# Four banks for the first expert product, the second kind's h2 rows from SBUF, expert numbers a block sooner, and one V row per 1.42 blocks

## The reference, cut to what matters

```python
q = (hc @ wq).reshape(T, PEER_HEADS, 2, PEER_KEY_DIM)
...
v1, i1 = lax.top_k(s1, PEER_TOPK)
v2, i2 = lax.top_k(s2, PEER_TOPK)
...
u_g = exp_u[e]
act = jax.nn.gelu(jnp.einsum('td,thkd->thk', hc, u_g).astype(jnp.float32), approximate=False)
w = (g * act).astype(hc.dtype)
return jnp.einsum('thk,thkd->td', w, exp_v[e])
```

## Time and profile before

| | us |
|---|---|
| median of 3 runs (819.38 to 820.77) | 820.61 |
| the profiled execution's own time | 820.81 |
| its span | 819.0 |
| PE matmul busy | 787.0 (96%) |
| DVE busy | 544.3 (66%) |
| GpSimd busy | 246.6 (30%) |
| ACT busy | 213.8 (26%) |
| chain that ended last: PE | 71% |
| chain that ended last: DMA | 21% |
| moved by DMA: 294.31 MB, mean rate | 359 GB/s |

### The profile page before, as it was taken

The page is one execution under the profiler, slowest core; times in us unless marked ns, Lnnn a source line. Parts: engine busy times, 40 slices in busy tenths (PEclk is TensorE's granted clock), DMA queues, the critical chain, the costliest instruction groups (busy, mean ns, idle before and its releaser), DMA issues.

```text
span 819.0 us, 14745 instructions
## 1 busy us (share of the span) xinstructions
PE 787.0 (96%) x5726; PEld 754.2 (92%) x5726; DVE 544.3 (66%) x1165; ACT 213.8 (26%) x604; POOL 246.6 (30%) x224
## 2 busy tenths in 40 slices
PE   6999999899998999979999999999999999999996
PEld 4988779889998999979999998899999999999995
DVE  4958879878999795658898996564434343443423
ACT  4464476551211121324554451100000000000004
POOL 2000000000005447325445654253434433443400
PEclk9999999999999999989999999999999999999998
DMA  8998973468978999999999999999999999999971
GB/s 332 406 378 328 388 308 155 194 238 322 393 314 267 397 392 383 350 351 388 409 409 408 409 408 408 406 407 409 409 409 409 406 409 408 409 408 409 409 279 52
DMA packets 77216, 294.31 MB, mean 359 GB/s; under 512 B 8799, under 2 KB 11103, under 8 KB 75868
## 3 DMA queue, kind: packets, MB, share of 16 engines
q1 hardware_dynamic: 48614, 191.52, 59.7%
q0 software_dynamic: 28000, 101.23, 31.8%
q10 hardware_dynamic: 534, 0.62, 0.2%
HBM read 291.25 MB, written 1.56 MB: 358 GB/s over the span
## 4 chain that ended last, share of the span: by engine, by line
PE 71%; DMA 21%; DVE 5%; ACT 1%; issue 1%; another core or an unknown queue 1%; SPq 0%; ACTq 0%; DVEq 0%
PE banks L1256 28%; PE banks L1286 23%; DMA raw<-in_v_b 13%; DMA raw<-in_u_t 5%; PE banks L1001 3%; PE banks L1269 2%; PE banks L919 2%; PE banks L954 2%; PE banks L997 2%; DMA raw<-in_w_mod 2%; PE banks L1070 1%; PE banks L924 1%; DVE sc_w L1396 1%; PE banks L970 1%; PE banks L1159 1%
## 5 line engine op out<-in xcount | busy, mean ns | idle before, releaser
L1256 PE MATMUL banks<-hT,raw 128*128 128x160 f32 x2048 | 290.4, 303 | 10.2 <-DMA raw<-in_u_t 6.6
L1256 PEld LDWEIGHTS banks<-hT,raw 128*128 128x128 f32 x2048 | 282.9, 192 | 13.2 <-DMA raw<-in_u_t 9.5
L1286 PE MATMUL banks<-act,raw 128*128 128x160 f32 x2048 | 285.5, 300 | 1.2 <-DMA raw<-in_v_b 0.2
L1286 PEld LDWEIGHTS banks<-act,raw 128*128 128x128 f32 x2048 | 279.2, 190 | 6.5 <-DMA raw<-in_v_b 5.8
L1764 DVE SCALAR_TENSOR_TENSOR row_sums<-rows,weight,row_sums 128x1024 f32<-128x1024 f32 x94 | 120.8, 1285 | 142.1 <-DMA rows<-in_v_b,idx 140.7
L574 POOL DMA_INDIRECT rows<-in_v_b,idx x96 | 119.9, 1249 | 170.5 <-PE banks L1286 111.8
L574 POOL DMA_INDIRECT rows<-in_u_rows,idx x96 | 118.8, 1237 | 153.1 <-DVE dots L1741 95.0
L1741 DVE CUSTOM_DVE_ANT_0 rows<-rows,h_rows 128x1024 f32<-128x1024 f32 x96 | 114.7, 1221 | 7.3 <-DMA rows<-in_u_rows,idx 6.5
L851 ACT ACTIVATE turned<-banks,ccol 128x256 f32<-128x256 f32 x8 | 3.8, 472 | 283.9 <-PE banks L1286 283.9
L555 POOL DMA_DIRECT2D h_lines<-h_stage x1 | 0.5, 519 | 204.5 <-ACT h_stage L822 204.5
L782 ACT ACTIVATE act<-banks 128x160 f32<-128x160 f32 (+19 forms) x118 | 31.3, 267 | 111.4 <-PE banks L1256 94.6
(11 more groups left out here) (245 smaller groups left out, 788.7 us busy)
## 6 DMA issues: line engine op xcount, KB each, us to landing
raw<-in_u_t SPq DMA_DIRECT2D x128, 512.0 KB, 10.7
raw<-in_v_b SPq DMA_DIRECT2D x128, 512.0 KB
wq<-in_wq SPq DMA_DIRECT2D x2, 4096.0 KB, 18.2
sh_w<-in_w_mod SPq DMA_DIRECT2D x8, 512.0 KB, 13.0
sc_w<-in_w_mod SPq DMA_DIRECT2D x8, 512.0 KB, 13.8
win<-in_w_in SPq DMA_DIRECT2D x8, 512.0 KB, 14.2
win<-in_w_in SPq DMA_DIRECT2D x1, 4096.0 KB, 20.9
sc_w<-in_w_mod SPq DMA_DIRECT2D x2, 2048.0 KB, 23.8
```

The costliest lines, as they stand in the source:

```text
L1256: last = nc.tensor.matmul(dst, raw[spot_of[n]][:, c * P:(c + 1) * P], hT[:, c, 0:MANY], start=(c == 0), stop=(c == DC - 1))
L1286: return nc.tensor.matmul(chunk_place(c)[:, 0:MANY], raw[spot_of[BLOCKS + j]][:, c * P:(c + 1) * P], act[:, j, :], start=(j == 0 and c < 4 ...
```

## The change

Five things are changed. (1) `u_bank(n)`: blocks 8 to 119 write banks 4, 5, 0, 1 in turn; a block waits for the GELU of the last block in its bank, that is n - 4, and blocks 10 and 11, the first in banks 0 and 1, wait for the copy that reads those banks (`xn_ready`). (2) The second kind's h2 rows no longer go by DRAM. ACT's queue copies the 32 rows from `h2_stage` four times, two copies after GELU 49 and two after GELU 51 (LATE_ROWS); the store on POOL's queue and the load on SP's queue are gone, with their waits. (3) EXPERTS_OUT is 16, one block sooner. (4) EXPERTS_IN is 17, two blocks sooner. (5) PACE is 1.42.

```diff
--- before.py
+++ after.py
@@ -52,9 +52,9 @@
 LAST = 4
 H2_AT = 2
 ROWS_AT = 48
-H2_LATER = (64,)
-EXPERTS_OUT = 17
-EXPERTS_IN = 19
+LATE_ROWS = (50, 52)
+EXPERTS_OUT = 16
+EXPERTS_IN = 17
 EXP_AT = 42
 SORT_SKIP = 4
 TURN_AT = 54
@@ -70,8 +70,9 @@
 PAIRS_AT = (0, 16, 40, 56)
 PAIRS_KEPT = 64
 PACE_FROM = 46
+FOUR_BANKS = (8, 120)
 AHEAD = 10
-PACE = 1.36
+PACE = 1.42
 PACE_U = 1.1
 BEFORE_TURN = 6
 BEFORE_GATES = 4
@@ -260,7 +261,6 @@
         banks = ctx.enter_context(nc.psum_tensor("banks", [P, 8, 512], F32))
         bank = [banks[:, n, :] for n in range(8)]
         scratch = nc.dram_tensor("bias_table", [MAPS, TABLE], F32, kind="Internal")
-        h2_lines = nc.dram_tensor("h2_lines", [FEW, D], F32, kind="Internal")
         expert_lines = nc.dram_tensor("expert_lines", [FEW, HK], U32, kind="Internal")
         gate_lines = nc.dram_tensor("gate_lines", [FEW, HK], F32, kind="Internal")
 
@@ -308,7 +308,7 @@
         block_used, act_out, late_act = map(sem, ("block_used", "act_out", "late_act"))
         second_ready, onehot_ready, gates_ready, gates_used, gates_out = map(
             sem, ("second_ready", "onehot_ready", "gates_ready", "gates_used", "gates_out"))
-        lines_moved, h2_saved = map(sem, ("lines_moved", "h2_saved"))
+        lines_moved = sem("lines_moved")
         gathered = [sem(f"gathered{n}") for n in range(SLOTS)]
         rows_used, weight_ready = map(sem, ("rows_used", "weight_ready"))
         peer_ready, chunk_out, columns_ready, x2_ready, final_ready, weighed = map(
@@ -402,6 +402,10 @@
 
             return (6, 4, 2)[(g - 2) % 3]
 
+
+        def u_bank(n):
+
+            return (4, 5, 0, 1)[n % 4] if FOUR_BANKS[0] <= n < FOUR_BANKS[1] else 4 + n % 2
 
         def gated_before(n):
 
@@ -511,14 +515,6 @@
                     sp.wait_ge(block_used, user_before[n] + 1)
                 sp.dma_start(raw[spot_of[n]][:, :], u_t[n] if n < BLOCKS else v_b[n - BLOCKS]
                              ).then_inc(raw_full[spot_of[n]], 16)
-                if n in H2_LATER:
-                    kind = 1 + H2_LATER.index(n)
-                    count = KINDS[kind]
-                    sp.wait_ge(h2_saved, 16)
-                    sp.wait_ge(block_used, ROWS_AT)
-                    sp.dma_start(h2_rows[kind][:, :],
-                                 bass.AP(tensor=h2_lines, offset=KIND_AT[kind] * D,
-                                         ap=[[0, P // count], [D, count], [1, D]])).then_inc(h2_late, 16)
             sp.dma_start(final_gb[:, :], final_g.broadcast_to([P, D])).then_inc(fin_in, 16)
             sp.wait_ge(final_ready, 1)
             sp.dma_start(out[0:P, :], xs[:, 0, :]).then_inc(out_done, 16)
@@ -551,8 +547,6 @@
             pool.wait_ge(table_built, 2 + len(LOG_BUCKETS))
             pool.dma_start(scratch.ap(), table[:, :]).then_inc(table_out, 16)
 
-            pool.wait_ge(xn_ready, TT + 3)
-            pool.dma_start(h2_lines.ap(), h2_stage[0:FEW, :]).then_inc(h2_saved, 16)
 
             pool.wait_ge(idx_in, 16 + 16 + 16 * len(KINDS))
             for i in range(GATHERS):
@@ -777,9 +771,9 @@
                 if before:
                     if n >= GATE_AT + 3:
                         sc.wait_ge(late_act, n - GATE_AT - 2)
-                    last = nc.scalar.activation(gelu_out[:, n % 2, 0:before], bank[4 + n % 2][:, 0:before], ACT.Gelu)
+                    last = nc.scalar.activation(gelu_out[:, n % 2, 0:before], bank[u_bank(n)][:, 0:before], ACT.Gelu)
                 if before < MANY:
-                    last = nc.scalar.activation(act[:, n, before:MANY], bank[4 + n % 2][:, before:MANY], ACT.Gelu)
+                    last = nc.scalar.activation(act[:, n, before:MANY], bank[u_bank(n)][:, before:MANY], ACT.Gelu)
                 last.then_inc(act_out, 1)
 
             def keep_gates(g):
@@ -827,6 +821,11 @@
                                      ).then_inc(h2_in, 16)
                 if group_at(n - 2 - GATE_AT) is not None:
                     keep_gates(group_at(n - 2 - GATE_AT))
+                if n in LATE_ROWS:
+                    count = KINDS[1]
+                    for q in range(LATE_ROWS.index(n) * 2, LATE_ROWS.index(n) * 2 + 2):
+                        sc.dma_start(h2_rows[1][q * count:(q + 1) * count, :], h2_stage[KIND_AT[1]:KIND_AT[2], :]
+                                     ).then_inc(h2_late, 16)
                 if n == EXPERTS_OUT:
                     sc.wait_ge(chosen_ready, 1)
                     sc.dma_start(expert_lines.ap(), e_u[FEW0:P, :]).then_inc(idx_in, 16)
@@ -1247,11 +1246,14 @@
 
             def u_block(n):
                 pe.wait_ge(raw_full[spot_of[n]], 16 * fills[n])
-                if n >= 2:
-                    pe.wait_ge(act_out, n - 1)
+                ahead = [m for m in range(n) if u_bank(m) == u_bank(n)]
+                if ahead:
+                    pe.wait_ge(act_out, ahead[-1] + 1)
+                elif n >= FOUR_BANKS[0]:
+                    pe.wait_ge(xn_ready, TT + 3)
                 if n == 0:
                     pe.wait_ge(q_sum, LISTS // 2 - 3)
-                dst = bank[4 + n % 2][:, 0:MANY]
+                dst = bank[u_bank(n)][:, 0:MANY]
                 for c in range(DC):
                     last = nc.tensor.matmul(dst, raw[spot_of[n]][:, c * P:(c + 1) * P], hT[:, c, 0:MANY],
                                             start=(c == 0), stop=(c == DC - 1))
@@ -1736,7 +1738,7 @@
                 if i == 0:
                     ve.wait_ge(h2_in, 16 + 16 * 2)
                 if i == KINDS[0]:
-                    ve.wait_ge(h2_late, 16 + 16 * len(H2_LATER))
+                    ve.wait_ge(h2_late, 16 + 16 * (P // KINDS[1]))
                 tile = row_tile(i)
                 nc.vector.tensor_tensor_reduce(out=tile, in0=tile, in1=h2_rows[kind_of(i)][:, :],
                                                scale=1.0, scalar=0.0, op0=ALU.mult, op1=ALU.add,
```

## The result

The changed kernel takes **814.53 us** (median of 9 runs, 810.82 to 816.11), the kernel before on the same chip 820.77 us (9 runs, 818.08 to 822.21). The ratio is 0.9923, with a 95% interval of 0.9909 to 0.9936: it is faster, by 6.2 us. The forecast was 804.7 us, with a range of 798 to 814: the sign was right, but 16.1 us were promised and 6.2 came, and the time lies just above the range.

A forecast was written before the change was run, and what follows sets the result against it. The prediction took DMA to bound the V half narrowly, with full engines from the twentieth slice on. Terms of 4.9 + 3.5 + 7.7 = 16.1 us gave 804.7 us; its own range was 801 to 809, widened to 798 to 814.

The forecast's parts named there:

- second kind's h2 rows, DMA time: U half, 340 to 355 us: removing the h2 load saves 5.4 us, copies lose at most 0.5; net 4.9 us.
- expert numbers and four banks, DMA time: U half: earlier gathers and PE's shorter GELU wait together save 3.5 us of DMA time, ends 0 and 4.5.
- how near the end of DMA the goal line comes: V's end: few_sums' start moves from 4.8 us behind DMA's end to 2.9 us before it, 7.7 us.
- behind the goal line: From few_sums' start to the end of the span: nothing changes, 22.05 us stay.
- the rival of late rows at 17.6 us: At few_sums: last gather lands in 17.6 us, PE idles 10.5 us, clock costs 2.5; 825.5 us, chance 0.05.
- one of the prediction's own signs of being wrong: U half: the forecast is wrong if the transfer rate dips again when the second kind's h2 copies run.
- the third term: V half: without the skew of some 7 us blocks land just in time, few_sums starts nearer DMA's end; 7.7 us.
- Behind it nothing is changed: The stretch after few_sums' start stays at 22.05 us to the end of the span.
- the first two terms: U half: 4.9 us of DMA time from the h2 rows, 3.5 us from expert numbers and four banks.
- PE-bound: Whole kernel: PE becomes the bound, having 23.3 us of losses to recover less 1.2; 798.7 us, chance 0.15.
- The slow stretch stays: 330 to 360 us: the load was not the cause, or copies cost the same; 813.7 us, chance 0.15.

The follow-up runs named there:

- h2_alone: The kernel before with only the second kind's h2 rows copied from SBUF, store and load removed: 814.0 us, ratio 0.9926.
- no_copies: The changed kernel without the second kind's four h2 copies, its dots using the first kind's h2 rows: 810.3 us, ratio 0.9883.
- no_v_rows: The changed kernel with V's row gathers left out from the eleventh on, each replaced by an 8 KB copy: 800.04 us, ratio 0.9769.
- experts_back: The changed kernel with the expert numbers stored and loaded at their old places, blocks 17 and 19: 815.89 us, ratio 0.9939.
- two_banks: The changed kernel with its u blocks in two banks again: 813.6 us, ratio 0.9918.
- last3: The changed kernel with three blocks instead of four kept back behind few_sums (LAST = 3): 806.35 us, ratio 0.9835.
- early_last3_136: The changed kernel with h2 copies at blocks 19 and 21, three blocks kept back behind few_sums, and PACE 1.36: 809.26 us, ratio 0.9881.
- pace_136: The changed kernel with PACE back at 1.36 instead of 1.42: 812.66 us, ratio 0.9911.
- rows_8_less: The changed kernel without the gathers and sums of V's last eight row tiles: 809.2 us, ratio 0.9864.
- before_last3: The kernel before with three blocks instead of four kept back behind few_sums: 819.77 us, ratio 1.0003.

## Why the prediction failed, step by step

Against the span of the profiled execution, 16.1 us were forecast and 7.7 came:

| step | forecast | measured | by |
|---|---|---|---|
| second kind's h2 rows, DMA time | 4.9 | 4.3 | before against h2_alone |
| expert numbers and four banks, DMA time | 3.5 | 1.5 | h2_alone (17.9) against the changed kernel (16.4) |
| how near the end of DMA the goal line comes | 7.7 | 3.3 | few_sums 4.8 us behind DMA's end, now 787.4 - 785.9 = 1.5 |
| behind the goal line | 0 | -1.9 | 23.9 against 22.05 us |

The four give 7.2 us; the other 0.5 is below what windows with whole GB/s and hundredths of a share resolve.

**Right.** The h2 load was the cause of the slow stretch and of the late block; 340 to 355 us is at 409 GB/s, and no u block is late. The first gather came at 248.2 us (forecast: near 249). PE does not wait on ACT at L1258, and its clock stays up from 200 us to the end of V's blocks. The wait at L1307 on DVE's last sum is 1.7 us (forecast 1 to 2), and the last gather took 8.2 us to land, as the 8.3 in the earlier trace rows said; the rival of late rows at 17.6 us is out.

**Two marks that were missed.** V's blocks were to be 2.19 us apart: 560 to 780 us has 1592/16 = 99.5 blocks in 220 us, 2.21 each, but the first 24 took 59.6 us, 2.48 each. And DMA was to be busy still when few_sums starts; it had run dry 1.5 us before.

**A size that was off.** The copies were to lose at most 0.5 us. No rate under 350 was only promised from 330 us on, but they run before that: over 310 to 330 us the nine kernels that have them at block 50 move 340 to 356 GB/s, the seven others 371 to 389. no_copies prices them at 1.9 us. So one of the prediction's own signs of being wrong, that the rate dips again when the copies run, did come. The trace leans to the Trainium skill's SBUF — State Buffer, "Door 1: The DMA port swizzle", against which the prediction decided: by it 32 partitions reach half of the ports, and 64 no more than 32, and the copies were 1.3 us dearer (an estimate of then). The row that decided was no witness. Over 210 to 226 us, in which the first kind's copies of 64 partitions run and land, the kernel before has 389 GB/s, but there the store to DRAM ran beside them; in the kernels without that store it is 365 to 372, in the changed one 372, 1.4 us short of the full rate. For the expert numbers it was the 3.5 us: what starts sooner was to use idle engine time one for one, and 4.9 us sooner brought 1.3. The banks brought nothing of their own, since the same change takes away the wait that they were to cover.

**The steps that failed** are two. The first is the third term, "How near the end of DMA the goal line can come": the sentence that the skew of some 7 us goes with the load and that without it "blocks land just in time". By its own sum block 120 starts 9.9 us ahead of the goal line, at 770.9 us; it started at 776.7. V blocks 2.19 us apart need 262.8 us for the first 120, and they took 272.1. Of the 9.3 us 7.0 were lost in the first 24, which took 59.6 us instead of 52.6. The 2.185 us count a row for every 1.42 blocks and leave out the ten rows that may go at V's start, 12.8 us of DMA time: blocks have half of the rate until they are in, 2.54 us each. In the kernel before, with the same ten rows, the 24 took 53.9 us; there PE came to V 15.6 us later. What the change gained shrinks accordingly: V's first block starts 15.6 us sooner (504.6 against 520.2), block 120 11.3, few_sums 9.6, and the end comes 7.7 us sooner. What DMA saved in the U half was there already in form of rows ahead, not of blocks ahead.

The other 2.3 us were lost by the later blocks, and there the skew is back. In the U half it did go (2 to 3 us between a block's first and last piece, where 12 to 13 stood before). In V it grows, to medians of 7 to 12 us, in every kernel that gathers rows there; in no_v_rows, which doesn't, it is gone. How much of the 2.3 us is the skew's, no run separates. In the kernel before it stood at 12 us from the load on, but the 17.6 us in the earlier trace rows would have come without the load too: in h2_alone, which has none, V blocks land 17 us after their issue. They were no evidence for what its removal brings. From block 120 on the sum was nearly right: few_sums 10.7 us later, where 9.9 was said.

The second is "Behind it nothing is changed", which put the stretch after few_sums at nothing, and with it the price of the wait ahead of it. A clock that falls there costs 1.7 us in the profiled execution. In that of experts_back it is dearer:

```profile
780.00:790.00 10.00, 7.97 (x57) 7.75 (x57) 3.85 (x3) 0.00 (x0) 0.00 (x0) 0.94 0.68 276
790.00:800.00 10.00, 10.00 (x47) 9.96 (x47) 0.00 (x0) 0.95 (x2) 0.00 (x0) 0.55 0.01 2
```

That is 1.2 + 9.0 = 10.2 us at the lower level, 5.1 us lost, behind a wait of 2.0 us. The prediction charged the clock for a wait of 10 us in its rival, and nothing for its own wait of 1.2. The runs at a mean clock of 0.990 to 0.992 suggest that the median of the changed kernel has the long form; the profiled one has the short. That would be why the median lies 1.35 us above the profiled execution, where it lay below in the kernel before. The profiled execution of two_banks, a kernel that takes the same time, shows what the long form looks like: 814.53 us, the changed kernel's median to the hundredth, at a mean clock of 0.992. There the first two terms give 7.2 us together, the third 4.2, and behind few_sums 5.1 are lost, the largest miss of the three. And last3, which takes the wait and the low clock away, runs at 806.35 us, inside the forecast's own 801 to 809.

**The rivals.** PE-bound (798.7 us) came true for the U half alone; with V's rows out, no_v_rows reached 800.04. "The slow stretch stays" gave 813.7 us, near the result, by a cause that the profile excludes: a time that fits is no proof. Two effects nearly cancel in it: U's gain, which it left out, and the losses in V and behind few_sums, which nobody had priced.

## What to carry to other kernels

Ask of each saving where the next reserve lies: this one removed 6 us of DMA time in the first half and the second half began with a queue of row gathers, so blocks had half of the rate just when they were needed. Where two queues share the engines, give the blocks' landing time with the other queue's traffic, not from the half in which it is light. And give the last transfer more cover than its time needs: with 1.7 us short, PE's wait and its clock ate up what the slower rate of rows brought: it is worth 4.8 us once the last row is covered (early_last3_136), and nothing while it isn't (pace_136); one block more of cover turned 6.2 us of gain into 13.5.

## What the runs showed of the hardware that was not expected

**The clock behind few_sums.** In the profiles it fell to 1.2 GHz there for 3.4 us (the changed kernel, pace_136) up to 10.2 us (experts_back), in eight kernels that keep four blocks back. It did not fall in the kernel before, in h2_alone and in no_v_rows, which keep four as well, nor in any of the five that keep three. A wait of 1.6 to 2.0 us goes before it in six of the eight, but pace_136 and rows_8_less have it with none, so the wait is not the whole cause. The waits of 1.9 to 2.0 us have the three stretches of 10.2 us behind them, those of 1.6 us the two of 6.8; the wait of 1.7 us and the two kernels without one have 3.4. What else decides stays open.

**A load that slows all.** The 512 KB load with a leading repeat of four lowered the rate of all queues together to 262 GB/s for 15 us at a DMA share of 1.03 (293 GB/s in before_last3), 5.4 us of DMA time; the same bytes as four copies out of SBUF cost 1.9 us. A share of 1.03 says that the engines are occupied, not that they move 409 GB/s.

**Saved time that doesn't add up.** Leaving 10.3 us of transfers out of V's end moved few_sums by 3.0 us, leaving out of U what cost 1.7 us there brought 3.3. Where PE's pace and DMA's are within 1 to 2%, as here (2.17 and 2.185 us per block), neither is the bound for long, and a sum of DMA time alone predicts little.
